# One layer of a hybrid decoder: w_out product with tokens on partitions, panels 2 and 3 loaded early, decode's small products regrouped

## The reference, cut to what matters

```python
h = _rms_norm(x, p['ln_mix_pre'])
qa, ka, va, qkvb, bb, ab, zb, qc, gates = jnp.split(h @ p['w_in'], _split_points(), axis=-1)
...
branches = jnp.stack([oa, ob, oc], axis=2)
up = jnp.einsum('blnc,ncd->blnd', branches, p['w_branch'])
gate = jax.nn.sigmoid(gates.reshape(Bsz, L, N_BRANCH, D_MODEL))
mix = jnp.sum(gate * up, axis=2) @ p['w_out']
x = x + _rms_norm(mix, p['ln_mix_post'])
h = _rms_norm(x, p['ln_ffn_pre'])
gt, uf = jnp.split(h @ p['w_ffn_in'], 2, axis=-1)
f = (jax.nn.silu(gt) * uf) @ p['w_ffn_out']
x = x + _rms_norm(f, p['ln_ffn_post'])
```

## Time and profile before

| what | value |
|---|---|
| three runs | 2187.46, 2189.09, 2193.29 us; median 2189.09 |
| the profiled execution's own time | 2202.99 us |
| its span | 2201.2 us |
| PE busy | 2106.1 us (96%) |
| PE weight load busy | 2056.9 us (93%) |
| DVE busy | 984.8 us (45%) |
| POOL busy | 770.8 us (35%) |
| ACT busy | 527.0 us (24%) |
| mean granted TensorE clock | 0.974 of full speed |

### The profile page before, as it was taken

One profiled execution on the slowest core, in us unless ns is written; L12 is line 12 of the kernel. 1 busy time (PEld: TensorE's weight loads), 2 busy tenths in 40 slices (PEclk: granted clock), 3 DMA queues, 4 the chain that ended last, 5 costly groups with the idle time before them and its releaser, 6 DMA issues.

```text
span 2201.2 us, 34799 instructions
## 1 busy us (share of the span) xinstructions
PE 2106.1 (96%) x13727; PEld 2056.9 (93%) x13727; DVE 984.8 (45%) x1666; ACT 527.0 (24%) x1161; POOL 770.8 (35%) x326
## 2 busy tenths in 40 slices
PE   6899999999999999999999997699999999999998
PEld 6899999999999999999899997699999999999997
DVE  5655540355555555311347902734353443534435
ACT  4233621233333333221032213400000000000002
POOL 2334874211111111121143434343434344344444
PEclk8999999999999999999799998799999999999999
DMA  4223332433122232253274323211111111111114
GB/s 156 88 77 98 117 107 98 132 98 98 58 75 82 81 98 64 70 170 100 88 256 161 107 81 110 101 49 48 48 38 48 48 48 42 44 48 39 55 39 158
DMA packets 227416, 193.82 MB, mean 88 GB/s; under 512 B 24715, under 2 KB 200459, under 8 KB 227298
## 3 DMA queue, kind: packets, MB, share of 16 engines
q1 hardware_dynamic: 213186, 182.72, 26.7%
q10 hardware_dynamic: 14128, 9.65, 1.4%
HBM read 146.26 MB, written 47.09 MB: 88 GB/s over the span
## 4 chain that ended last, share of the span: by engine, by line
PE 85%; DVE 7%; ACT 4%; DMA 2%; issue 1%; POOL 1%; SPq 0%; ACTq 0%; DVEq 0%; POOLq 0%
PE psum L1402 23%; PE psum L918 13%; PE psum L1469 11%; PE psum L1016 7%; PE psum L1088 6%; PE psum L1168 4%; PE psum L1412 4%; PE psum L1394 4%; PE psum L1137 2%; ACT pr L1739 1%; PE psum L1126 1%; DMA brw<-s_br 1%; PE psum L971 1%; PE psum L940 1%; PE psum L1110 1%
## 5 line engine op out<-in xcount | busy, mean ns | idle before, releaser
L807 POOL TENSOR_TENSOR wsp<-raw,kc 128x1024 fp32r<-128x1024 f32 x137 | 329.7, 2407 | 1362.3 <-PE psum L1088 433.9
L1402 PE MATMUL psum<-actD,wsp 128*128 128x352 f32 x3168 | 517.7, 324 | 0.9 <-DVE actD L2435 0.9
L1402 PEld LDWEIGHTS psum<-actD,wsp 128*128 128x128 f32 x3168 | 511.5, 189 | 1.0 <-DVE actD L2435 1.0
L810 POOL TENSOR_TENSOR wsp<-raw,wsp 128x1024 fp32r<-128x1024 f32 x137 | 343.5, 2508 | 10.7
L918 PE MATMUL psum<-actT,wsp 128*128 128x352 f32 (+1 forms) x1800 | 295.7, 325 | 6.5 <-POOL wsp L810 6.5
L918 PEld LDWEIGHTS psum<-actT,wsp 128*128 128x128 f32 (+1 forms) x1800 | 285.7, 186 | 12.2 <-POOL wsp L810 6.8
L2484 DVE TENSOR_TENSOR accT<-accT,psum 128x352 f32<-128x352 f32 x504 | 241.7, 520 | 50.1 <-PE psum L1469 50.1
L1469 PE MATMUL psum<-fT,wsp 128*128 128x352 f32 x1512 | 249.8, 323 | 0.4 <-DVE accT L2484 0.4
L1469 PEld LDWEIGHTS psum<-fT,wsp 128*128 128x128 f32 x1512 | 244.0, 188 | 0.7 <-DVE accT L2484 0.7
L1088 PE MATMUL psum<-actT,wsp 128*128 128x352 f32 x1152 | 216.4, 333 | 0.0
L2467 DVE TENSOR_TENSOR fr<-psum,sg 128x352 f32<-128x352 f32 x66 | 34.6, 524 | 378.7 <-PE psum L1402 375.9
(11 more groups left out here) (406 smaller groups left out, 2403.5 us busy)
## 6 DMA issues: line engine op xcount, KB each, us to landing
raw<-in_w_in SPq DMA_DIRECT2D x100, 256.0 KB, 3.9
raw<-in_w_ffn_in SPq DMA_DIRECT2D x88, 256.0 KB, 3.1
gat<-s_gate SPq DMA_DIRECT2D x12, 1056.0 KB, 5.1
raw<-in_w_ffn_out SPq DMA_DIRECT2D x44, 256.0 KB, 2.7
s_gate<-gst SPq DMA_DIRECT2D x48, 176.0 KB, 1.8
s_qkv<-y SPq DMA_DIRECT2D x12, 528.0 KB, 3.0
brw<-s_br SPq DMA_DIRECT2D x3, 2112.0 KB, 9.9
raw<-in_w_branch SPq DMA_DIRECT2D x24, 256.0 KB, 5.6
```

Source lines behind the costliest of these rows:

```text
L807: pool.tensor_tensor(wsp[:, slot, 0], raw[:, slot], ones.unsqueeze(1).to_broadcast([P, KT, P]), ALU.mult).then_inc(w_hi, 1)
L810: pool.tensor_tensor(wsp[:, slot, 1], raw[:, slot], wsp[:, slot, 0].bitcast(F32), ALU.subtract).then_inc(w_lo, 1)
L1402: mm = pe.matmul(psum[:, bank, 0:CH], wsp[:, slot, a, k, :], actD[:, h, k, CH * c:CH * c + CH], start=(k == 0 and q == 0), stop=(k == KT - ...
```

## The change

In the beginning SP issues panels 2 and 3 right after the loads of x. Panel 2 is split into `wm`, a buffer that the memory panels use later. The chunks of panels 0 and 1 get banks of their own (`FIRST_BANK`), so most of them wait for no emptying, and the turning of the convolution state moves behind `first_chunk(0, 2)`. Panel 2 has its own loop on PE that reads `wm`.

```diff
+    FIRST_BANK = (0, 1, 2, 7, 0, 1)
@@ block.sync
         sp.dma_start(xin[:, 0:2, :], mem_view...).then_inc(x_in[0], 16)
+        load_b(2)
+        load_b(3)
...
         sp.wait_ge(p_in, 96)
-        for n in range(2, 4):
-            load_b(n)
@@ block.gpsimd
-        split_at(2, 0, 64, 6 + 5)
+        pool.wait_ge(w_in[0], 64)
+        pool.tensor_tensor(wm[:, 0], raw[:, 0], ones.unsqueeze(1).to_broadcast([P, KT, P]), ALU.mult).then_inc(w_hi, 1)
+        pool.wait_ge(w_hi, 3)
+        pool.tensor_tensor(wm[:, 1], raw[:, 0], wm[:, 0].bitcast(F32), ALU.subtract).then_inc(w_lo, 1)
         split(3, 1, 64)
@@ block.tensor
             if t == 6:
-                first_chunk(1, 0, 3 + 1)
+                first_chunk(1, 0, 3)
...
-        first_chunk(0, 2, 3)
-        first_chunk(1, 2, 3 + 5)
-        gemm(2, 0)
+        first_chunk(0, 2, 3 + 1)
...
+        first_chunk(1, 2, 3 + 2)
+        pe.wait_ge(w_lo, 2 + 3)
+        for c in range(3):
+            pe.wait_ge(g_ev, 3 + (5, 6, 6)[c])
...
+                    mm = pe.matmul(psum[:, c, 0:CH], wm[:, a, k], actT[:, h, k, CH * c:CH * c + CH],
```

```diff
         for b in range(DB):
-            gate_mm(18)
-            mem_scores(b)
+            gate_mm(6)
             if b + 1 < DB:
                 mem_keys(b + 1)
+            gate_mm(6)
+            mem_scores(b, 6)
...
-        update(0)
-        update(1)
-        gate_mm(8)
-        update(2)
-        gate_mm(6)
-        mem_values(4)
-        gate_mm(14)
+        for j in range(3):
+            update(j)
+            gate_mm(5)
+        mem_values(4, 5)
+        gate_mm(5)
```

```diff
+    UF = UO
+    W_SEQ = [("b", j) for j in range(5)] + [("o", 0), ("b", 5), ("o", 1), ("b", 6), ("o", 2), ("b", 7), ("b", 8), ("b", 9), ("o", 3),
+             ("b", 10), ("o", 4), ("b", 11), ("o", 5), ("o", 6), ("o", 7)]
@@ block.gpsimd
+                if j in (5, 6):
+                    pool.wait_ge(b_lo, 1 + MIX_N(0, (1, 3)[j - 5]) + 1)
+                if j == 7:
+                    pool.wait_ge(g_mm, 6 + UO)
+                split_to(W_N[kind, j], *(wo_part(j, a) for a in range(2)))
+        split_at(NPF, NPF % 2, 32 * (NPF // 2) + 32, 6 + UO - 6)
+        for t in range(NT):
+            add_row(pool, t, t % 2, P)
@@ block.tensor
+        def out_rows(t, slot, rows):
+            pe.wait_ge(t_y, t + 1)
+            c = (P * t + rows - 1) // CH
+            for k in range(KT):
+                if t == 0:
+                    pe.wait_ge(w_lo, W_N["o", k] + 3)
+                if t in (0, 2, 5):
+                    pe.wait_ge(b_lo, 1 + MIX_N(c, k) + 1)
                 for q, (a, h) in enumerate(passes):
+                    for half in range(2):
+                        mm = pe.matmul(psum[0:rows, 2 * slot + half, :], actD[:, h, (k + 4) % 8, P * t:P * t + rows],
+                                       wo_part(k, a)[:, 512 * half:512 * half + 512],
+                                       start=(k == 0 and q == 0), stop=(k == KT - 1 and q == 2))
             mm.then_inc(t_tr, 1)
+        pe.wait_ge(g_ev, 3 + UO)
+        for t in range(NT + 1):
+            out_rows(t, t % 2, P if t < NT else NS)
             if t >= 2:
+                turn_back(t - 2, t % 2, P)
+        pe.wait_ge(w_lo, NPF + 3)
+        for c in range(2):
+            pe.wait_ge(u_lo, 2 + 3 * c + 3)
+            full_chunk(NPF % 2, c, 6 + c)
+        turn_back(NT - 1, 1, P)
+        turn_back(NT, 0, NS)
@@ block.vector
         norms(NT - 1, 1, first=NS)
+        dve.wait_ge(t_x1, NT)
+        add_row(dve, NT, 0, NS)
```

More of the change, by code:

```diff
@@ L933, in first_chunk @@
         def first_chunk(n, c, read):
+            bank = FIRST_BANK[2 * c + n]
             pe.wait_ge(w_lo, n + 3)
@@ L1233, in mem_scores @@
             for h in range(4):
+                if h == 2:
+                    gate_mm(gap)
                 for t in range(2):
```

227 lines of the change are left out of this document (120 added, 107 removed).

## The result

| | before | changed |
|---|---|---|
| median of the runs | 2191.19 us (2187.46 to 2202.86) | 2162.42 us (2158.18 to 2165.76) |
| ratio | | 0.9854, 95% interval 0.983 to 0.9878 |
| span of the profiled execution | 2201.2 us | 2162.6 us |

The changed kernel is faster: by 28.8 us between the medians, by 32.0 us by the ratio, and by 26.7 to 37.2 us by its interval.

What follows compares the result with a forecast made beforehand. PE, busy for 96% of the span, was taken as the bound. From the profiled 2203.0 us, 13 (beginning), 12.3 (decode) and 19.7 (w_out and ladder) gave 2158.0; less 2 to 3 for the profile's excess, 2156 us, range 2137 to 2180.

Steps and rivals of the forecast that it cites:

- Beginning, -13: Start of the kernel: panel 2 follows panel 1 without its stall and first chunks wait less, about 13 us, between 7 and 17.
- The second rival: Beginning: DVE's convolution sets the pace, so 3 us are gained instead of 13; 2166 us, chance 0.07.
- w_out and ladder, -19.7: First branch matmul to the FFN's chunk 2: 310.8 us become 291.1, with bounds of -30 and -6.
- wait for the banks: Ahead of the w_out product: PE waits until the branch banks are empty and the mix is split, 12 us, bounds 8 and 15.
- tail: After the last product tile: some 2.5 ladder rounds remain before the next full chunk, 16.3 us, bounds 13 and 22.
- The branch stage's term of +6.5: Branch stage: 14 more POOL split instructions slow DVE's additions and cost PE 0.48 us each; bounds 0 and 15.
- Decode, -12.3: Decode: regrouped small products keep the clock up, leaving 10 of 37.5 us at half clock; bounds 0 and -16.8.
- A clock of 0.5 in decode: Decode: a clock of 0.5 in any slice of the profile after would show the prediction wrong.
- the clock in decode gains nothing: Decode: the clock falls elsewhere instead, say in the updates, so 12.3 us less is gained; 2168 us, chance 0.10.
- the one on DVE as the bound: Branch stage: each of POOL's 14 instructions blocks a DVE addition throughout, +20 to +30 for PE; 2170 to 2180 us, chance 0.09.
- The slower one: Decode: the clock falls and stays down, all 576 gate matmuls at half clock, +58 us; 2228 us, chance 0.04.
- The last one: w_out product: matmuls sharing a stationary operand lose the 13.6 ns overhead, so it takes 92 us or less; 2150 us, chance 0.02.

Runs made afterwards that it cites:

- the w_out run: The kernel before with only the new w_out product (tokens on partitions, parts ready early, ladder in its shadow): 2170.7 us, ratio 0.9897.
- the late splits: The changed kernel, with POOL splitting w_out's parts 6 and 7 only after the branch stage's last bank is empty: 2150.5 us, ratio 0.9812 against before.
- the scores alone: The kernel before with only decode's scores, window keys and small products up to the memory's turned rows regrouped: 2198.5 us, ratio 1.0009.

## Why the prediction held, point by point

**Beginning, -13.** Right in kind, small by 1.7: 14.7 us in the rows, -15.6 or -13.8 in the run with this part alone. The second rival did not come: DVE's convolution did not set the pace, since the whole gain was still there at the first prompt tile.

**w_out and ladder, -19.7.** Alone this part measured -22.4. The profiles give 290.8 us from the first branch matmul to the third FFN chunk, where the sum had 291.1; term by term:

| term | predicted | measured | from |
|---|---|---|---|
| branch stage | 157.0 | 157.7 | window |
| wait for the banks | 12 | 10.95 | timeline |
| 432 matmuls | 98.1 | 100.4 | 9 tiles of 11.16 (1270.78 to 1281.94) |
| turns between them | 5.2 | 4.8 | six of 0.80 |
| restart of the clock | 2.5 | 1.9 | first tile 13.08 less 11.16 |
| tail | 16.3 | 14.8 | window |

The closeness is partly luck. The branch stage's term of +6.5 had the right size and the wrong mechanism. It charged PE for every addition that POOL stretches. The additions did grow, to 1155 ns, but of the +7.6 us next to nothing lies in the last 396 matmuls, where POOL had seven instructions more: 4.1 us came up to the restart at the third panel (37.6 us from the first branch matmul instead of 33.5) and 3.5 in the 288 matmuls behind it, with the clock that fell there. In the w_out run the same three stretches have 2.2, 2.7 and 0.0 us more than before. With that stop gone the stage took 149.9. The regrouped updates, which the prediction costed only inside decode, added 5 us to this stage in the kernel before, but only some 1.5 beside the w_out part (157.7 against 156.2 with decode as before). The 12 us of waiting were right in size, and the text gave the rests of the mix and POOL's splits as two things side by side. They are one thing, as the late splits show: POOL stretches the rests from 1.82 to 7.83 us. The 512-column product took 232.5 ns and not 227. The Trainium skill's formula in "TensorE: Matmul & The Clock Gate", section "Back-to-back issue gap", would give 215.8, an estimate from that page; the section calls it the gap of an isolated matmul, where the prediction wrote back-to-back. Here the measurement decides. The 2.1 us behind the tail, where the clock comes up, was forgotten: the restart was counted after the first wait and not after the second. The tail's own gap of PE was 4.1 us (3.19 + 0.93), where the prediction had about 8.

**Decode, -12.3.** This is the step that failed, in the size of the term and in a premise. The sentence is "With no row of small products longer than about one us, I take 10 of the 37.5 us as kept". It was right about the places: the updates had clock 1.00, and the rest of the fall stood around the window keys. But there a row of over two us was left, and the fall grew. PE in the changed kernel:

```profile
985.82 0.95 PE L1301 MATMUL psum<-da,ckT 128*128 128x4 f32 x8
986.70 0.29 PE L1335 MATMUL psum<-kc,dxt 32*32 32x32 f32 x4
986.92 1.06 PE L1345 MATMUL psum<-da,wkT 64*128 64x16 f32 x8
987.91 1.50 PE L1232 MATMUL psum<-actT,wsp 128*128 128x352 f32 x6
...
991.72 2.13 PE L1232 MATMUL psum<-actT,wsp 128*128 128x352 f32 x6
```

That row takes 2.1 us (985.82 to 987.91), and from 990 to 1000 the clock is 0.50. A clock of 0.5 in decode was one of the prediction's own signs of being wrong. On the mean of the changed profiles 17 us are kept, not 10. And the 37.5 (41 by the window of all of decode) were those of one execution: with the same decode, six other profiles had 14 to 29. Alone, the regrouping measured 0 to +9 us. The rival "the clock in decode gains nothing" (chance 0.10) had the effect about right and the place wrong: it looked for the new falls in the updates, which had none. The clock is lost again around the window keys, some 1.6 us go apart from the clock, and the branch stage gives back more.

**Why the number was still near.** The sum ran against the profiled execution, 13.9 us over the median, and the decode term of -12.3 in effect took that excess away. Had the decode term been 0 and the excess been taken off in full, the sum would be 2203.0 - 13 - 19.7 - 13.9 = 2156.4. Two ways lead to the same number. The text chose the one whose mechanism was wrong, so the closeness here is luck, but it did name the link ("part of the 13.9 us ... is surely the 24 us at half clock in the updates").

The other rivals: the one on DVE as the bound did not come, although the additions did grow, to 1155 ns. Its 14 x 2.1 us doesn't follow from its own words, since 2.6 less 0.82 is 1.8 and makes 25 us and not 29; its range is little touched. The slower one, a clock that stays down, did not come in any of the profiles with small pieces: the longest time at half clock was 22 us, and 29 with the scores alone. The last one, by which the 13.6 ns vanish where two matmuls share the stationary operand, did not come either: 19.2 ns stand above the columns, and in the product's stretch 480 matmuls (six turns among them) had 481 weight loads. The range took the 6.4 us easily.

## What to carry over

One profile of a kernel whose clock falls at chance moments is a sample: before costing a clock term from it, see how far that execution lies from the median, and take the excess as the first candidate for the same time. Give a regrouping a window for each of its parts: here one half took the fall away and the other lengthened its own, and the time of the whole showed neither. When a stage is made shorter, look at the first wait of the next one, since what was hidden by the length (here probably a load and its splitting) comes out there. And when work is moved to an idle engine that shares operand paths with a busy one, look at what the busy one does in those very microseconds: here a split held back by one line was worth some 10 us, and a sigmoid ahead of a wait, with its inputs half a panel later, some 8, both by the rows.

## What was not expected of the hardware

That the time of one DVE instruction with both operands in SBUF goes from 0.45 us to 2.0 or 2.4 beside POOL, in a row of four 1.82 us to 7.83 and 9.67. In the longer of these rows DVE got about one such instruction for each of POOL's four (2.2 to 2.6 us). What a matmul of 512 columns costs here, 232.5 ns at clock 1.00, is 19.2 ns above its columns, against 13.6 for one of 352; the runs don't show why. And with identical instructions in decode, the time at half clock varied between 14 and 41 us over seven profiles. That is worth 12 us. The runs of the kernel before lay between 2187.3, at a mean clock of 0.984, and 2208.4, at 0.973.
